# Moving a chunk's down projection between the next chunk's gate and up projections

## The chip, the core and the metric

The kernel runs on one core of a Trainium2 chip. The metric is the device time of one execution in microseconds; lower is better. The engines are named PE (matmul, its weight loads as PEld), DVE (vector), ACT (scalar), POOL (GpSimd) and SP (which issues the loads of weights).

## What is computed

Two blocks follow each other on 512 tokens of 1024 features, in float32. The first has two layers of recurrence, latent attention and memory attention; the second has a feed-forward network, a mixer of neighbourhood attention and pooling, a second feed-forward network and a gated side input. The change touches only the two feed-forward networks:

```python
D_FF = 2816

def swiglu(x, w_gate, w_up, w_down):
    return (jax.nn.silu(x @ w_gate) * (x @ w_up)) @ w_down

def second_block(...):
    f = swiglu(rms_norm(h, ffn1_pre_g[i]), ffn1_w_gate[i], ffn1_w_up[i], ffn1_w_down[i])
    h = h + 0.5 * rms_norm(f, ffn1_post_g[i])
    ...
    f = swiglu(rms_norm(h, ffn2_pre_g[i]), ffn2_w_gate[i], ffn2_w_up[i], ffn2_w_down[i])
    h = h + 0.5 * rms_norm(f, ffn2_post_g[i])
```

## The kernel before

**Precision by splitting.** Every operand is kept as a high and a low part (`xh`, `xl`; `wh`, `wl`), and a product is three matmuls: high by high, high by low, low by high (lines 902 to 904).

**Blocks, pieces, units.** A plan is written out once as a list, and every engine walks through it in order. A `Block` is one projection. Its weights come in units of up to four tiles of 128 rows; its output lies in PSUM banks 0 to 3 (`bank`), and a piece is one unit times one bank, up to 4 x 3 = 12 matmuls. A gate or up block ("tr": the weights are stationary, the activations move) has two units; with 512 columns it has four banks and eight pieces, with 256 columns two banks and four pieces. A down projection is two blocks ("nat": the activations are stationary, the weights move) of one unit and four pieces each, one for each half of the output features. A bank that is filled again waits until the block before has been read out of it (`prior`).

**How weights come.** SP loads a unit into one of two buffers `raw`, ACT casts it to `wh` (line 1255, three buffers) and POOL subtracts the cast from it, which gives `wl` (line 851). ACT casts the unit that is two places ahead of the piece it has come to (`prepare`), and only when the unit before that piece's is over on PE.

**The networks.** The 2816 inner columns are cut into six chunks of 512, 256, 512, 512, 512 and 512 columns. Below, G0 to G5, U0 to U5 and D0 to D5 are their gate, up and down projections. ACT evacuates G with a SiLU to `SG` (line 1276). DVE evacuates U bank by bank in three steps (`times_gate`): the product with `SG` (line 1651), its cast to the high part (line 1652), the low part by subtraction (line 1653). These parts are the stationary operand of D; they are kept in `yh`, `yl` for even chunks and in `zh`, `zl` for odd ones. DVE adds D's banks up in `facc` (line 1647, shown as `side`). A D waits for all evacuations of its U (`need`, by the semaphore `dve_evac`). D0 starts at bank 2 in place of bank 0 (`shift`).

**The order before** is G0 U0 G1 U1 D0 G2 U2 D1 G3 U3 D2 G4 U4 D3 G5 U5 D4, and then D5 within the phase `norm`, in which the root mean square of the sum is taken and the result is transposed (line 1157) for the next block. ACT, DVE and PE enter such a phase by `settle_before`, a wait for all evacuations of the blocks ahead of it.

Of the kernel before, what the change touches and what calls it, by code (L numbers as in the profile page):

```python
# [302 lines left out]
def build(nc, x, x_t, mem_t, positions, w_in, w_uq, w_uk, w_uv, w_mk, w_mv, w_out, ln_g, ln_b, cols_in,  # L303
# [3 lines left out]
    with ctx:  # L307
# [111 lines left out]
        def w_cols(w, row0, ktiles, c0, width):  # L419
            return w[row0:row0 + ktiles * P, c0:c0 + width].rearrange("(k p) n -> p k n", p=P)  # L420

        plan = []
        add = plan.append
# [14 lines left out]
        def norm(first, last_blocks, pre=None, turned=True, scale=1.0, second=True, by_columns=False):  # L438


            _, at = norm_order(first, pre, turned)
            ph = Phase("norm", *(len(o) for o in at), slots=T + 1, writes="x" if turned else None, mode=first,
                       gain=pre, tiles=2 if turned else 0, scale=scale, layer=second)
            ph.by_columns = by_columns
            if len(last_blocks) == 2:
                last_blocks[1].shift = 2
            if first == "layer":

                between, *ends = (b.pieces() for b in last_blocks)
                for b, at in zip(last_blocks, ((0, 1, 0, 1), (2, 2, 0, 2), (3, 3, 1, 3))):  # L450
                    b.shift, b.at = 0, at
                ph.slots[0], ph.slots[2] = between[:2], between[2:]
                for n in range(T):
                    ph.slots[n + 1] += [pieces[n] for pieces in ends]
                add(ph)
                return
            for b in last_blocks:
                pieces = b.pieces()
                ph.slots[0] += pieces[:-T]
                for n in range(T):  # L460
                    ph.slots[n + 1].append(pieces[n - T])
            add(ph)
# [99 lines left out]
        def load_gains(post, pre=None):  # L562
            pairs = [(gain2_b[:, 0, :], post_gains[post:post + 1, :].partition_broadcast(P))]
            if pre is not None:
                pairs.append((gain2_b[:, 1, :], pre_gains[pre:pre + 1, :].partition_broadcast(P)))
            add(Load(*pairs))

        def ffn(wg, wu, wd, gains, by_columns=False):

            widths = [512, D_FF % 512] + [512] * (D_FF // 512 - 1)  # L570
            chunks = [(sum(widths[:i]), width) for i, width in enumerate(widths)]

            def down(i):
                c, width = chunks[i]
                blocks = [Block(w_cols(wd, c, width // P, n * 512, 512), width // P, 512, "nat", f"ff{i % 2}",
                                "accumulate", "dve", (n, i == 0)) for n in range(2)]
                if i == 0:

                    for b in blocks:
                        b.shift = 2  # L580
                return blocks

            for i, (c, width) in enumerate(chunks):
                add(Block(w_cols(wg, 0, KD, c, width), KD, width, "tr", "x", "silu", "act", SG, banks=width // P))
                add(Block(w_cols(wu, 0, KD, c, width), KD, width, "tr", "x", "times_gate", "dve", i % 2,
                          banks=width // P))
                if i == 0:
                    load_gains(*gains)
                else:
                    for b in down(i - 1):  # L590
                        add(b)
            norm("post", down(len(chunks) - 1), pre="work2", scale=0.5, by_columns=by_columns)

        ffn(f1g, f1u, f1d, (0, 1), by_columns=True)


# [48 lines left out]
        add(Phase("turned", writes="x"))  # L645
        norm("post", last[2:], pre="work2")
        ffn(f2g, f2u, f2d, (2, 3))

        load_gains(3)
# [36 lines left out]
        for e in plan:  # L686
# [4 lines left out]
            if isinstance(e, Late):  # L691
                b = e.block
# [12 lines left out]
            for piece in (e.pieces() if isinstance(e, Block) else [pc for slot in e.slots for pc in slot]):  # L705
                b, unit, j = piece
# [1506 lines left out]
```

How the kernel before makes its waits and increments, by code:

```python
        def wait(eng, semaphore, value):  # L757
            if value > 0:
                eng.wait_ge(semaphore, value)
# [1 line left out]
        def units_over(eng, n):  # L761
            if n > 0:
                eng.wait_ge(*unit_end[n - 1])
# [46 lines left out]
        @block.sync  # L811
# [14 lines left out]
                if u == 10:  # L826
                    sp.dma_start(xs[:, :, :], x.rearrange("(t p) n -> p t n", p=P)).then_inc(x_loaded, 16)
                if u >= 2:
                    wait(sp, low_done, low_upto[u - 1][0])
                    wait(sp, low_done_dve, low_upto[u - 1][1])
                sp.dma_start(raw[:, u % 2, 0:nk, 0:b.width], b.w[:, k0:k0 + nk, :]).then_inc(raw_loaded[u % 2], 16)
            for t in range(T):
                for n in range(2):
                    sp.wait_ge(dve_step, finish.dve + 2 + 2 * t + n)
                    cut = slice(n * 512, (n + 1) * 512)
                    sp.dma_start(out[t * P:(t + 1) * P, cut], xs[:, t, cut]).then_inc(stored, 16)
            sp.wait_ge(stored, 16 * 2 * T)
# [2 lines left out]
        @block.gpsimd  # L842
        def _(pool):
            for u, (b, k0, nk) in enumerate(units):
                for k in range(nk):
                    if low_on_dve(u, k):
                        continue
                    pool.wait_ge(high_done, tiles_upto[u] + k + 1)
                    s = (slice(None), u % 3, k, slice(0, b.width))
                    pool.tensor_tensor(wl[s], raw[:, u % 2, k, 0:b.width], wh[s].bitcast(F32),
                                       ALU.subtract).then_inc(low_done, 1)
```

## Time and profile before

| | us |
|---|---|
| median of 3 runs | 2118.03 |
| lowest and highest run | 2116.44, 2118.12 |
| span of the profiled execution | 2113.3 |
| PE busy | 2089.2 |
| DVE busy | 894.8 |
| POOL busy | 868.0 |
| ACT busy | 789.8 |

The page gives the span of the profiled execution, from its first to its last instruction, and not its whole time. Busy times are shares of that span; the four engines run side by side. A matmul's busy time in the trace includes the time in which it drains, so that matmuls in a row overlap: their price is read from the distance between two starts.

### The profile page before, as it was taken

How to read it: one execution, taken by the hardware profiler on the slowest of the kernel's cores; microseconds unless marked ns; L12 is line 12 of the kernel's file. 1: busy time of each engine (PE TensorE's matmuls, PEld its weight loads, DVE VectorE, ACT ScalarE, POOL GpSimd, SP SyncE). 2: the span in 40 equal slices, each digit the busy share in tenths (PEclk: the TensorE clock that was granted, in tenths of full speed). 3: DMA queues.
4: the chain of work that ended last, by engine and by line, in shares of the span. 5: the costliest groups of instructions: out<-in, count | busy, mean ns of one | idle time of the engine just before them, and what ended most of it. 6: DMA issues, size and time to landing. Idle time of an engine off the chain costs nothing.

```text
span 2113.3 us, 33496 instructions
## 1 busy us (share of the span) xinstructions
PE 2089.2 (99%) x13820; PEld 1741.6 (82%) x13820; DVE 894.8 (42%) x1653; ACT 789.8 (37%) x1611; POOL 868.0 (41%) x680
## 2 busy tenths in 40 slices
PE   8999999999999999999999999999999999999998
PEld 7878888778978888778888888888888888888886
DVE  6173565535373465526432211433422612222264
ACT  5424335554423325455422222345433432222244
POOL 4633433232543433233354444343444345454423
PEclk9999999999999999999999999999999999999999
DMA  7522223122222223122242332242233133332222
GB/s 247 178 65 80 78 67 100 41 80 80 80 82 80 77 68 100 41 81 70 76 144 83 118 98 83 89 135 80 66 114 100 61 110 101 109 108 92 100 70 90
DMA packets 98679, 196.65 MB, mean 93 GB/s; under 512 B 3680, under 2 KB 12256, under 8 KB 98144
## 3 DMA queue, kind: packets, MB, share of 16 engines
q1 hardware_dynamic: 95072, 183.25, 26.6%
q10 hardware_dynamic: 3456, 11.27, 1.5%
q8 instruction: 109, 1.79, 0.3%
q14 instruction: 42, 0.34, 0.1%
HBM read 192.41 MB, written 2.10 MB: 92 GB/s over the span
## 4 chain that ended last, share of the span: by engine, by line
PE 59%; ACT 1%; DVE 0%; issue 0%; DVEq 0%
PE ps L902 18%; PE ps L903 18%; PE ps L904 18%; PE ps L1017 1%; PE ps L1157 1%; PE ps L1025 0%; PE ps L1034 0%; PE ps L1180 0%; PE ps L1200 0%; PE ps L1189 0%; PE ps L1070 0%; PE ps L1052 0%; ACT L1581 0%; PE ps L974 0%; PE ps L1210 0%; PE ps L1062 0%
## 5 line engine op out<-in xcount | busy, mean ns | idle before, releaser
L851 POOL TENSOR_TENSOR wl<-raw,wh 128x512 fp32r<-128x512 f32 (+2 forms) x676 | 867.8, 1307 | 1220.6 <-ACT wh L1255 1210.8
L1255 ACT CAST wh<-raw 128x512 fp32r<-128x512 f32 (+2 forms) x692 | 380.7, 604 | 773.3 <-PE ps L904 672.8
L902 PE MATMUL ps<-xh,wh 128*128 128x512 f32 (+1 forms) x1376 | 514.2, 374 | 1.2 <-issue 1.2
L904 PE MATMUL ps<-xh,wl 128*128 128x512 f32 (+1 forms) x1376 | 509.1, 370 | 0.0
L903 PE MATMUL ps<-xl,wh 128*128 128x512 f32 (+1 forms) x1376 | 508.7, 370 | 0.0
L902 PEld LDWEIGHTS ps<-xh,wh 128*128 128x128 f32 x1376 | 259.4, 189 | 46.1 <-issue 3.9
L904 PEld LDWEIGHTS ps<-xh,wl 128*128 128x128 f32 x1376 | 259.1, 188 | 44.6
L903 PEld LDWEIGHTS ps<-xl,wh 128*128 128x128 f32 x1376 | 259.4, 188 | 42.1
L902 PE MATMUL ps<-wh,xh 128*128 128x512 f32 (+1 forms) x608 | 239.1, 393 | 0.2 <-issue 0.2
L904 PE MATMUL ps<-wh,xl 128*128 128x512 f32 (+1 forms) x608 | 234.4, 386 | 0.0
L903 PE MATMUL ps<-wl,xh 128*128 128x512 f32 (+1 forms) x608 | 234.4, 385 | 0.0
L902 PE MATMUL ps<-wh,yh 128*128 128x512 f32 x496 | 198.0, 399 | 0.2
L904 PE MATMUL ps<-wh,yl 128*128 128x512 f32 x496 | 193.6, 390 | 0.0
L903 PE MATMUL ps<-wl,yh 128*128 128x512 f32 x496 | 193.4, 390 | 0.0
L1651 DVE TENSOR_TENSOR work<-ps,work 128x512 f32<-128x512 f32 x44 | 30.3, 688 | 383.3 <-PE ps L904 383.3
L902 PEld LDWEIGHTS ps<-wh,xh 128*128 128x128 f32 x608 | 114.2, 188 | 22.6 <-issue 1.4
L904 PEld LDWEIGHTS ps<-wh,xl 128*128 128x128 f32 x608 | 114.2, 188 | 21.8
L903 PEld LDWEIGHTS ps<-wl,xh 128*128 128x128 f32 x608 | 114.3, 188 | 20.4 <-issue 0.2
L902 PEld LDWEIGHTS ps<-wh,yh 128*128 128x128 f32 x496 | 93.3, 188 | 20.5 <-POOL wl L851 0.8
L904 PEld LDWEIGHTS ps<-wh,yl 128*128 128x128 f32 x496 | 93.1, 188 | 19.9
L903 PEld LDWEIGHTS ps<-wl,yh 128*128 128x128 f32 x496 | 93.3, 188 | 18.5
L1647 DVE TENSOR_TENSOR side<-side,ps 128x512 f32<-128x512 f32 x88 | 59.3, 686 | 106.0 <-PE ps L904 103.4
(273 smaller groups left out, 2436.2 us busy)
## 6 DMA issues: line engine op xcount, KB each, us to landing
raw<-w_in SPq DMA_DIRECT2D x58, 1024.0 KB, 5.2
raw<-w_out SPq DMA_DIRECT2D x20, 1024.0 KB, 5.0
raw<-f1g SPq DMA_DIRECT2D x10, 1024.0 KB, 5.1
raw<-f1u SPq DMA_DIRECT2D x10, 1024.0 KB, 5.1
raw<-f1d SPq DMA_DIRECT2D x10, 1024.0 KB, 5.0
raw<-f2g SPq DMA_DIRECT2D x10, 1024.0 KB, 5.2
raw<-f2u SPq DMA_DIRECT2D x10, 1024.0 KB, 5.1
raw<-f2d SPq DMA_DIRECT2D x10, 1024.0 KB, 5.1
```

Source lines behind the costliest of these rows:

```text
L851: pool.tensor_tensor(wl[s], raw[:, u % 2, k, 0:b.width], wh[s].bitcast(F32), ALU.subtract).then_inc(low_done, 1)
L902: pe.matmul(o, still[0], move[0], start=k0 + k == 0, stop=False)
L903: pe.matmul(o, still[0], move[1], start=False, stop=False)
L904: mm = pe.matmul(o, still[1], move[0], start=False, stop=k0 + k == b.ktiles - 1)
L1017: mm = pe.matmul(ps[:, 4 + h, 0:width], q_heads[:, 2 * p + h, cut], k_heads[:, p, h, 0:width], start=True, stop=True)
L1157: mm = pe.transpose(ps[:, 4 + 2 * (t % 2) + b, f * P:(f + 1) * P], src[:, t, (4 * b + f) * P:(4 * b + f + 1) * P], ident[:, :])
L1255: act.copy(wh[:, v % 3, k, 0:width], raw[:, v % 2, k, 0:width]).then_inc(high_done, 1)
L1647: ins = dve.tensor_copy(dst, src) if first else dve.tensor_tensor(dst, dst, src, ALU.add)
L1651: link(dve.tensor_tensor(tmp, src, SG[:, j, :], ALU.mult))
```

## The change

In the loop over chunks, D of the chunk before is added behind the gate projection in place of behind the up projection. The order becomes G0 U0 G1 D0 U1 G2 D1 U2 G3 D2 U3 G4 D3 U4 G5 D4 U5, and then D5 within the norm. Blocks, pieces, banks, units and buffers stay as they are; only their order changes, on every engine that walks through the plan.

```diff
             for i, (c, width) in enumerate(chunks):
                 add(Block(w_cols(wg, 0, KD, c, width), KD, width, "tr", "x", "silu", "act", SG, banks=width // P))
+                for b in down(i - 1) if i else ():
+                    add(b)
                 add(Block(w_cols(wu, 0, KD, c, width), KD, width, "tr", "x", "times_gate", "dve", i % 2,
                           banks=width // P))
                 if i == 0:
                     load_gains(*gains)
-                else:
-                    for b in down(i - 1):
-                        add(b)
             norm("post", down(len(chunks) - 1), pre="work2", scale=0.5, by_columns=by_columns)
```

In the following rows a name pair is output, moving operand, stationary operand. The new file is one line shorter ahead of the matmuls, so lines 902 to 904 become 901 to 903. PE at the end of the first network, where D5 (`zh`, `zl` stationary) begins, before:

```order
L902 MATMUL ps<-wh,yh 128x512
L903 MATMUL ps<-wl,yh 128x512
L904 MATMUL ps<-wh,yl 128x512
L902 MATMUL ps<-wh,zh 128x512 [waits low_done,dve_evac]
L903 MATMUL ps<-wl,zh 128x512
```

and with the change:

```order
L901 MATMUL ps<-xh,wh 128x512
L902 MATMUL ps<-xl,wh 128x512
L903 MATMUL ps<-xh,wl 128x512
L901 MATMUL ps<-wh,zh 128x512 [waits low_done,dve_evac]
L902 MATMUL ps<-wl,zh 128x512
```

Before, the last matmuls of D4 stand ahead of D5's first; now the last ones of U5 do, whose evacuations write `zh` and `zl`.

PE behind U1, the up projection with two banks, before (the last three matmuls of U1, the first two of D0, which begins on bank 2):

```order
L902 MATMUL ps<-xh,wh 128x512
L903 MATMUL ps<-xl,wh 128x512
L904 MATMUL ps<-xh,wl 128x512
L902 MATMUL ps<-wh,yh 128x512 [waits low_done,dve_evac]
L903 MATMUL ps<-wl,yh 128x512
```

and with the change (the last three of U1, the first two of G2, which begins on bank 0):

```order
L901 MATMUL ps<-xh,wh 128x512
L902 MATMUL ps<-xl,wh 128x512
L903 MATMUL ps<-xh,wl 128x512
L901 MATMUL ps<-xh,wh 128x512 [waits dve_evac,low_done,dve_step,act_step]
L902 MATMUL ps<-xl,wh 128x512
```

D0 has moved ahead of U1, and G2 follows U1 directly, on the two banks that U1 has just filled.

## Rows read from the trace of the kernel before

**Rows 1.** The page's first part: busy us, share of the span, instructions.

```profile
PE 2089.2 (99%) x13820; PEld 1741.6 (82%) x13820; DVE 894.8 (42%) x1653; ACT 789.8 (37%) x1611; POOL 868.0 (41%) x680
```

**Rows 2.** Both networks: stretch, length, busy PE, PEld, DVE, ACT, POOL, clock, DMA.

```profile
1015.00:1357.00 342.00, 342.00 (x1604) 286.59 (x1604) 89.14 (x124) 87.96 (x168) 163.00 (x133) 1.00 0.32 102
1683.00:2025.00 342.00, 342.00 (x1603) 286.64 (x1604) 89.34 (x123) 88.12 (x168) 163.18 (x133) 1.00 0.31 102
```

**Rows 3.** PE's timeline: start, us, instruction. First matmuls of U1 and of D0.

```profile
1072.31 0.39 PE L902 MATMUL ps<-xh,wh 128*128 128x512 f32 x1
...
1083.19 0.39 PE L902 MATMUL ps<-wh,yh 128*128 128x512 f32 x1
```

**Rows 4.** DVE's timeline: U1's two banks, U5's last bank, D4's last; brackets: idle before.

```profile
1080.77 0.69 DVE L1651 TENSOR_TENSOR work<-ps,work 128x512 f32<-128x512 f32 x1 [17.26 <-PE ps L904]
1081.50 1.29 DVE L1652 CAST zh<-work 128x512 fp32r<-128x512 f32 x1
1082.82 1.66 DVE L1653 TENSOR_TENSOR zl<-work,zh 128x512 fp32r<-128x512 f32 x1
...
1086.22 1.66 DVE L1653 TENSOR_TENSOR zl<-work,zh 128x512 fp32r<-128x512 f32 x1
...
1334.68 0.69 DVE L1651 TENSOR_TENSOR work<-ps,work 128x512 f32<-128x512 f32 x1 [0.79 <-PE ps L904]
1335.41 0.43 DVE L1652 CAST zh<-work 128x512 fp32r<-128x512 f32 x1
1335.87 1.67 DVE L1653 TENSOR_TENSOR zl<-work,zh 128x512 fp32r<-128x512 f32 x1
...
1356.45 0.69 DVE L1647 TENSOR_TENSOR side<-side,ps 128x512 f32<-128x512 f32 x1 [2.04 <-PE ps L904]
```

**Rows 5.** PE's timeline: the first matmul of D4, one within the norm phase.

```profile
1334.48 0.39 PE L902 MATMUL ps<-wh,yh 128*128 128x512 f32 x1
...
1381.03 0.36 PE L902 MATMUL ps<-xh,wh 128*128 128x256 f32 x1 [0.44 <-issue]
```

**Rows 6.** DVE's timeline: cast and subtraction of a bank of U0.

```profile
1054.30 0.43 DVE L1652 CAST yh<-work 128x512 fp32r<-128x512 f32 x1
1054.76 0.69 DVE L1653 TENSOR_TENSOR yl<-work,yh 128x512 fp32r<-128x512 f32 x1
```

**Rows 7.** POOL's timeline: subtractions in a row, around U1 and at D4's start.

```profile
1073.69 10.24 POOL L851 TENSOR_TENSOR wl<-raw,wh 128x512 fp32r<-128x512 f32 x8 [1.42 <-ACT wh L1255]
...
1335.44 5.75 POOL L851 TENSOR_TENSOR wl<-raw,wh 128x512 fp32r<-128x512 f32 x4 [5.67 <-ACT wh L1255]
```

**Rows 8.** ACT's timeline: casts at D4's start, and those in the norm phase.

```profile
1334.74 2.19 ACT L1255 CAST wh<-raw 128x512 fp32r<-128x512 f32 x4 [8.70 <-PE ps L904]
...
1357.45 2.18 ACT L1255 CAST wh<-raw 128x512 fp32r<-128x512 f32 x4 [9.64 <-issue]
```

**Rows 9.** Timeline of DVE and PE: a matmul elsewhere that waited for DVE.

```profile
973.68 0.69 DVE L1878 TENSOR_TENSOR work<-ps,work 128x512 f32<-128x512 f32 x1 [0.62 <-PE ps L1070]
...
974.51 0.45 PE L1070 MATMUL ps<-work,side 128*128 128x256 f32 x1 [0.34 <-DVE work L1878]
```

**Rows 10.** PE's timeline at the kernel's start.

```profile
7.95 0.58 PE L902 MATMUL ps<-yh,wh 128*128 128x256 f32 x1 [7.95 <-POOL wl L851]
8.32 0.42 PE L903 MATMUL ps<-yl,wh 128*128 128x256 f32 x1
...
16.16 0.38 PE L902 MATMUL ps<-yh,wh 128*128 128x256 f32 x1
16.37 0.28 PE L903 MATMUL ps<-yl,wh 128*128 128x256 f32 x1
16.49 0.28 PE L904 MATMUL ps<-yh,wl 128*128 128x256 f32 x1
```

**Rows 11.** Windows at the kernel's end, columns as in rows 2.

```profile
2105.00:2106.00 1.00, 0.97 (x5) 0.47 (x3) 0.29 (x1) 0.95 (x4) 0.00 (x0) 1.00 0.23 86
2108.00:2109.00 1.00, 0.00 (x0) 0.00 (x0) 1.00 (x2) 0.46 (x3) 0.00 (x0) 0.86 0.00 0
```

## The prediction

> **What bounds the kernel now.** I read the page's first part for the busiest engine, then the windows over the two feed-forward networks, then the timelines of PE, DVE and POOL at the two places where the new order puts blocks side by side that were apart.
>
> PE is busy for 2089.2 of 2113.3 us [rows 1]. In the two windows that hold the networks, from the first matmuls of the gate projection to the first ones of the last down projection, it is busy for 342.00 of 342.00 us, both times, at a granted clock of 1.00 [rows 2]. That is the main fact: where the change acts, PE does not wait at all. Weight loads, casts on ACT, subtractions on POOL and evacuations on DVE are all hidden behind matmuls. A reordering there cannot shorten anything that PE waits for; it can only keep PE full or open gaps. The number and the shapes of the matmuls stay what they are: U1 runs from 1072.31 to 1083.19 [rows 3], 48 matmuls at 0.2267 us, so a piece of 12 takes 2.72 us, and I take the same price for it in its new place.
>
> So the question is which new neighbours make PE wait. I call G, U and D the gate, up and down projection of chunk i, and T the moment at which an up projection's last piece is over and the next block's first matmul starts in the trace of before.
>
> **Edits that cost nothing, and their cover.** D(i-1) behind G(i) needs all four (or two) evacuations of U(i-1); in the new order a whole G lies between them, 21.8 us for a chunk of 512 and 10.9 us for the one of 256 (that of U1). DVE ends the last of them about 2 us after U's end, so this is covered several times over. U(i) behind D(i-1) starts on a bank that was filled three pieces before; behind the shifted D0 its first bank was filled one piece, 2.72 us, earlier, and a down evacuation takes 0.69 us [rows 4]. G(i+1) behind a four-bank U(i) starts on a bank that was filled three pieces, 8.2 us, before. The units keep their sizes, and each is still cast while the unit two places ahead of it runs; the two short units of G1 and the two of U1 now stand apart, which gives SP's loads, ACT's casts and POOL's subtractions more room, not less. No instruction is added on any queue, and the load of gains stays behind U0. Sum: 0.
>
> **Term 1: D5 directly behind U5 (both networks).** D5's first matmul waits for all four evacuations of U5, since its stationary operand is what they write. Before, D4 with 21.8 us lay between. Now the last bank's evacuation is exposed. In the trace U5 ends at T = 1334.48 [rows 5]; DVE takes up bank 3 at 1334.68, its product lasts 0.69, its cast starts at 1335.41 and its subtraction at 1335.87 [rows 4]. The start was set by PE (DVE had been idle for 0.79 us before it), so this start stays. The subtraction took 1.67 us there. Where POOL is idle it takes 0.69 [rows 6], and POOL had begun four subtractions at 1335.44 [rows 7]. That burst belongs to the unit that ACT began to cast at 1334.74, as soon as D4 began [rows 8]. In the new place the next unit belongs to the block behind the norm, and ACT reaches it only when the norm phase's settling wait is over, that is after the last evacuation of the block ahead: in before this is seen as the cast at 1357.45 [rows 8], 0.31 us behind the end of D4's last evacuation (1356.45 + 0.69) [rows 4]. So POOL will not be running and I take 0.69: bank 3 is ready at 1335.87 + 0.69 = 1336.56, T + 2.08. From DVE's end to PE's start I take 0.14 us (973.68 + 0.69 = 974.37 to 974.51) [rows 9], and 0.15 us because the first matmul after a wait has its weight load exposed (7.95 to 8.32 is 0.37 where the spacing is 0.21) [rows 10]. Term 1 is 2.08 + 0.14 + 0.15 = 2.37 us per network. Its bounds: 2.2 without the last surcharge, 3.4 if POOL runs after all (1.67 in place of 0.69).
>
> **Term 2: G2 directly behind U1 (both networks).** U1 has only two banks. Behind it, D0 used its two other banks first; G2 uses bank 0 first, which was filled one piece, 2.72 us, before U1's end. In the trace U1 ends at T = 1083.19 [rows 3]. DVE starts bank 0 at 1080.77, but the cast takes 1.29 and the subtraction 1.66, so that it ends at 1084.48, T + 1.29 [rows 4]; the second network shows the same pattern. The reason is POOL: it ran eight subtractions from 1073.69 for 10.24 us, to 1083.93 [rows 7], 1.28 each, while the same cast and subtraction take 0.43 and 0.69 where it is idle [rows 6]. Is POOL there in the new order too? The casts for the two units of G2 start when the two units of U1 start, as those for D0's did: a burst of four from about U1's start + 1, another from its second unit's start + 1 (1072.31 + 5.44 + 0.96 = 1078.7) to about 1083.8. The second burst lies on bank 0's evacuation as before, so I take the measured end. G2 then starts at T + 1.29 + 0.14 + 0.15 = T + 1.58 in place of T. Its second piece needs bank 1 at T + 1.58 + 2.72 = T + 4.30. In before bank 1 was ready at 1086.22 + 1.66 = 1087.88, T + 4.69 [rows 4], with the handing over T + 4.98: 0.68 more. POOL's third burst is shorter in the new order (D1's unit has two tiles, not four), so bank 1 may come up to 0.5 us earlier; I take half of the 0.68. Term 2 is 1.58 + 0.34 = 1.92 us. Its bounds: 0, if DVE has POOL out of its way (1.88 us of work from 1080.77 end at 1082.65, ahead of T), and 2.3.
>
> The Trainium skill (SBUF — State Buffer, "Who interferes with whom") says that DVE and GpSimd share a port pair, which whoever starts first keeps for the whole instruction while the other waits. By that rule a cast and a subtraction could each have to sit out one whole POOL subtraction of 1.28 us, in place of the 0.86 and 0.97 us seen here; bank 0 would end 0.73 us later, and the sum, as an estimate by that page, would be 2 x 0.73 = 1.5 us more. What the trace has is in between, as it should be where the second engine comes while the first is under way.
>
> **Sum.** 2.37 + 1.92 = 4.29 us per network, 8.6 us for two. The page gives the span of the profiled execution, 2113.3 us, and not its own time; the median of the three runs is 2118.03, 4.7 us above, which I take for what lies around the span. I add to the median: 2126.6 us, 0.4% slower. The bounds of the terms give 2 x 2.2 = 4.4 and 2 x 5.7 = 11.4: 2122.4 to 2129.4.
>
> **Rivals.** *Only the last wait is left, not slower.* If POOL's second burst in U1 ends ahead of bank 0's cast (the point is 1081.50 on the clock of before, T - 1.69), or starts behind it, term 2 is 0. Term 1 leaves 4.7 us, and if the norm behind D5 swallows its own short wait (0.44 us on PE [rows 5]) it gives back 0.9: 2118.0 + 4.7 - 0.9 = 2121.8, within 0.2%, which is about what a measurement of this kernel can tell from no change (4.2 us, the line at 2122.3). Without the gift it is 2122.7. For it: the neighbouring units change, and POOL's bursts follow them. Against it: the burst hangs on the start of U1's second unit, which keeps its distance to the bank.
>
> *The clock falls.* At the start of the kernel, after 7.95 us of idle PE, matmuls of 256 columns are spaced 0.21 us until 16.37 and 0.12 after it [rows 10], the two levels of 1.2 and 2.4 GHz. At the end, PE stops at 2106 and the granted clock is 0.86 in the slice from 2108 to 2109 [rows 11]. PE would be idle for about 2.1 us in front of D5. If that were enough, up to 8.4 us would run at half speed, up to 4 us lost per network; with half of it 2126.6 + 4 = 2130.6. Against it: the clock still held more than 2 us behind PE's last matmul.
>
> The Trainium skill (TensorE: Matmul & The Clock Gate, "A second HAM failure mode: psum-queue depth-cycling") tells of a kernel whose short PE pauses between groups of matmuls made the clock swing between its two levels. By it the new waits, which are such pauses, would cost the price of this rival. The trace speaks against it: the windows that hold the networks are at 1.00, but they hold no pause either.
>
> *A gain.* It would need PE time to win back, and there are 0.00 us of it in 684 [rows 2]. I keep a small chance for what I don't see. That the change does nothing is excluded by PE's order.
>
> **How the numbers follow.** Forecast, both waits: 0.72, 2124 to 2129.4. Only the last wait: 0.15, 2121.8 to 2122.8. The clock: 0.09, 2129 to 2134. A gain: 0.04. Predicted 2126.6. For 8 in 10 the range reaches from 2121.8 to 2130.2; it leaves out the gain and most of the clock's case. Slower by over 0.2%: 0.72 + 0.09 + a little over a quarter of the second case, 0.85; within 0.2%: 0.11; faster: 0.04.
>
> **What would show it.** PE's waits of the new profile should hold two waits on DVE of about 2 us at the first matmul of D5, behind the up projection's subtraction, and two of about 1.3 us at G2's first matmul, perhaps two short ones at its second piece; PE's busy time in the networks unchanged; clock 1.00. Wrong would be: no wait at G2 (second case), a wait at D5 well over 2.5 us (POOL was there), matmuls behind it spaced wider than 0.23 us (the clock), or a PE wait on POOL or on a load anywhere in the networks, which would mean that the order of units matters after all.

## The result and the profile after

The changed kernel takes 2124.89 us (median of 4 runs, 2124.29 to 2127.45) against 2117.24 us for the kernel before on the same chip (4 runs, 2116.24 to 2118.12): ratio 1.0042, 95% interval 1.0029 to 1.0056. It is slower by 0.4%, as forecast (2126.6, range 2121.8 to 2130.2). A second, larger comparison gave 1.0043 (below).

PE's waits of the changed kernel, longest in total first (what it waited for: us in total, times, longest):

```profile
PE ps L901 <- POOL wl L850: 9.0, 3, 7.6
PE ps L901 <- DVE zl L1652: 6.7, 4, 2.0
PE ps L1093 <- DVE work L1942: 2.5, 2, 1.3
```

The second line is new: four waits for the up projection's subtraction, which the kernel before has not at all. They are the two forecast ones, once in each network. PE's idle time in the networks, 0.00 us before [rows 2], is 3.3 us in each now (346.00 less 342.67 and 342.68; the windows are 4 us longer because the networks are, and the idle time is the waits' 1.36 + 1.97):

```profile
1015.00:1361.00 346.00, 342.67 (x1603) 286.16 (x1602) 89.46 (x122) 88.98 (x169) 161.88 (x134) 1.00 0.31 101
1687.00:2033.00 346.00, 342.68 (x1601) 286.21 (x1600) 89.78 (x123) 88.74 (x169) 161.86 (x134) 1.00 0.31 101
```

**G2 behind U1.** DVE's timeline (start, us, instruction, idle before) around the end of U1 in the first network:

```profile
1102.13 0.69 DVE L1650 TENSOR_TENSOR work<-ps,work 128x512 f32<-128x512 f32 x1 [7.57 <-PE ps L903]
1102.86 1.27 DVE L1651 CAST zh<-work 128x512 fp32r<-128x512 f32 x1
1104.17 1.65 DVE L1652 TENSOR_TENSOR zl<-work,zh 128x512 fp32r<-128x512 f32 x1
...
1107.28 1.66 DVE L1652 TENSOR_TENSOR zl<-work,zh 128x512 fp32r<-128x512 f32 x1
```

POOL's at the same time:

```profile
1100.07 5.20 POOL L850 TENSOR_TENSOR wl<-raw,wh 128x512 fp32r<-128x512 f32 x4 [0.41 <-ACT wh L1254]
1105.51 2.88 POOL L850 TENSOR_TENSOR wl<-raw,wh 128x512 fp32r<-128x512 f32 x2 [0.24 <-ACT wh L1254]
```

PE's, with U1's last matmul, G2's first, and the step to G2's second piece (1109.00):

```profile
1104.33 0.39 PE L903 MATMUL ps<-xh,wl 128*128 128x512 f32 x1
1106.08 0.47 PE L901 MATMUL ps<-xh,wh 128*128 128x512 f32 x1 [1.36 <-DVE zl L1652]
1106.38 0.40 PE L902 MATMUL ps<-xl,wh 128*128 128x512 f32 x1
...
1108.69 0.39 PE L903 MATMUL ps<-xh,wl 128*128 128x512 f32 x1
1109.00 0.50 PE L901 MATMUL ps<-xh,wh 128*128 128x512 f32 x1
1109.33 0.40 PE L902 MATMUL ps<-xl,wh 128*128 128x512 f32 x1
```

Cast and subtraction of U1's bank 0 are as slow as before [rows 4], POOL's second burst lies over them as before [rows 7], and bank 0 is ready at 1104.17 + 1.65 = 1105.82. G2 starts 0.26 us later. Without a wait it would have started at 1104.33 + 0.227 = 1104.56, so the start is 1.52 us late; the first matmul takes 0.07 more than usual. The second piece starts 0.08 late (0.31 us behind the matmul before it, in place of 0.23), since bank 1 was ready only at 1107.28 + 1.66 = 1108.94, and its first matmul takes 0.10 more than usual; the third burst was short, as the order of units said. The rest is spread thinly: behind its first matmul, the matmuls of G2's first piece are 0.231 us apart in place of 0.227. Over the 144 matmuls of U1 and G2 the trace holds 1.86 us more than 144 x 0.2267 us, and 1.87 in the second network.

**D5 behind U5.** The last bank of U5 on DVE:

```profile
1357.90 0.69 DVE L1650 TENSOR_TENSOR work<-ps,work 128x512 f32<-128x512 f32 x1 [0.79 <-PE ps L903]
1358.62 0.43 DVE L1651 CAST zh<-work 128x512 fp32r<-128x512 f32 x1
1359.08 0.69 DVE L1652 TENSOR_TENSOR zl<-work,zh 128x512 fp32r<-128x512 f32 x1
```

and PE, with U5's last matmul and D5's first two:

```profile
1357.47 0.39 PE L903 MATMUL ps<-xh,wl 128*128 128x512 f32 x1
1359.83 0.50 PE L901 MATMUL ps<-wh,zh 128*128 128x512 f32 x1 [1.97 <-DVE zl L1652]
1360.17 0.39 PE L902 MATMUL ps<-wl,zh 128*128 128x512 f32 x1
```

POOL is out of the way here: ACT begins the next unit's cast at 1360.08 and POOL its subtractions at 1360.78, both behind the evacuation, which therefore takes 0.69 at its last step in place of 1.67 [rows 4]:

```profile
1360.78 5.05 POOL L850 TENSOR_TENSOR wl<-raw,wh 128x512 fp32r<-128x512 f32 x4 [7.80 <-ACT wh L1254]
```

The evacuation ends at 1359.77; PE starts at 1359.83, 2.13 us behind the free slot at 1357.70, and spends 0.11 more than usual on the first matmul: 2.24 us.

**The clock, in the second network only.** Windows of 1 us around D5's start there (stretch, length, busy of PE, PEld, DVE, ACT and POOL, granted clock, DMA):

```profile
2030.00:2031.00 1.00, 0.08 (x1) 0.00 (x0) 0.85 (x2) 0.00 (x0) 0.00 (x0) 1.00 0.00 0
2031.00:2032.00 1.00, 0.00 (x0) 0.00 (x0) 0.96 (x2) 0.00 (x0) 0.00 (x0) 1.00 0.00 0
2032.00:2033.00 1.00, 0.95 (x2) 0.83 (x3) 0.00 (x0) 0.70 (x2) 0.00 (x1) 0.52 0.00 0
2033.00:2034.00 1.00, 1.00 (x4) 0.73 (x3) 0.00 (x0) 1.00 (x3) 1.00 (x1) 0.50 0.00 0
2034.00:2035.00 1.00, 1.00 (x4) 0.81 (x3) 0.00 (x0) 0.48 (x1) 1.00 (x2) 0.50 0.00 0
2035.00:2036.00 1.00, 1.00 (x4) 0.80 (x4) 0.00 (x0) 0.00 (x0) 1.00 (x2) 0.77 0.00 0
2036.00:2037.00 1.00, 1.00 (x6) 0.79 (x5) 0.21 (x1) 0.00 (x0) 1.00 (x2) 1.00 0.00 0
```

and PE's timeline within it:

```profile
2032.05 0.79 PE L901 MATMUL ps<-wh,zh 128*128 128x512 f32 x1 [1.97 <-DVE zl L1652]
...
2033.07 0.63 PE L903 MATMUL ps<-wh,zl 128*128 128x512 f32 x1
2033.50 0.63 PE L901 MATMUL ps<-wh,zh 128*128 128x512 f32 x1
```

The granted clock falls to 0.5, the lower of its two levels (1.2 GHz), as the matmuls come back after a wait of 1.97 us, and stays there for 3.4 us; matmuls are 0.43 us apart in place of 0.23. The first 60 matmuls of D5 take 1.64 us more than 60 x 0.2333, of which 0.11 is the first one: the fall costs 1.53 us. In the first network the same wait, to the hundredth, left the clock at 1.00 (D5 starts at 1359.83):

```profile
1360.00:1361.00 1.00, 1.00 (x5) 0.82 (x6) 0.00 (x0) 0.92 (x2) 0.22 (x1) 1.00 0.00 0
```

Together: 1.86 + 1.87 + 2 x 2.24 + 1.53 = 9.7 us in the networks. The span grew by 9.2 (2113.3 to 2122.5); the kernel reached the first network 0.4 us earlier in this execution than in the one before.

### The profile page after: what moved, and what is told of

It is laid out like the page before. It is cut to its first block, busy times and chain, and to the rows that moved or that the text cites. A ratio compares the mean times of both kernels' runs of the same rounds, so it can differ in the third digit from the quotient of the medians.

```text
span 2122.5 us, 33496 instructions
## 1 busy us (share of the span) xinstructions
PE 2091.6 (99%) x13820; PEld 1741.3 (82%) x13820; DVE 895.0 (42%) x1653; ACT 790.0 (37%) x1611; POOL 866.0 (41%) x680
## 4 chain that ended last, share of the span: by engine, by line
PE 58%; DVE 1%; ACT 1%; issue 0%; DVEq 0%
PE ps L901 18%; PE ps L902 18%; PE ps L903 18%; PE ps L1016 1%; PE ps L1156 1%; PE ps L1024 0%; PE ps L1033 0%; PE ps L1179 0%; PE ps L1199 0%; PE ps L1188 0%; PE ps L1069 0%; PE ps L1051 0%; DVE zl L1652 0%; ACT L1580 0%; PE ps L973 0%
```

## The experiments

The theory was: the new order costs nothing by itself; it exposes two evacuations in each network, U1's (bank 0, slowed by POOL) in front of G2 and U5's in front of D5, and behind D5's wait the clock may fall. The rivals were that every moved D costs a little, that POOL has nothing to do with U1's evacuation, that something other than these evacuations holds PE, and that the new order has a gain that the waits hide. The cover of an evacuation, below, is the time that other matmuls fill between it and the block that needs it. All ratios are to runs of the kernel before on the same chip, with a 95% interval behind them; a difference in us is worked out from the ratio. Line numbers shift a little from kernel to kernel.

**The changed kernel again** (label e1_again).

> The changed kernel once more, as the yardstick for the others. Theory (each network loses 1.9 us at G2, which waits for U1's evacuation, and 2.2 us at D5, which waits for U5's; on top of it the clock falls behind one of the D5 waits for 1.5 us): 7 to 9.5 us slower than the kernel before, and four waits of PE on the up projection's subtraction, two of 1.3 to 1.4 and two of about 2.0 us. If the fall of the clock is a matter of chance, it may be behind the first network's D5 this time, behind both, or behind none.

2124.51 us (5 runs) against 2116.00 (24 runs), ratio 1.0043, interval 1.0030 to 1.0055: 9.1 us. The four waits were there with the same lengths, and the clock fell behind neither D5. It did fall elsewhere: at 48 us, in the first block's start, where PE had waited 2.39 us for weights (see the last section).

**D4 alone back** (e2_last_back).

```diff
-                for b in down(i - 1) if i else ():
+                for b in down(i - 1) if i and i not in (5,) else ():
                     add(b)
                 add(Block(w_cols(wu, 0, KD, c, width), KD, width, "tr", "x", "times_gate", "dve", i % 2,
                           banks=width // P))
+                for b in down(i - 1) if i in (5,) else ():
+                    add(b)
```

> D4 alone goes back behind U5; D0 to D3 stay in their new places. Theory: the two waits in front of D5 are gone, and with them the fall of the clock; what stays is the wait at G2, 2 x 1.9 = 3.7 us slower than the kernel before (3 to 5). Rival, that the new order costs by itself (every D between G and U a little): 6 or more.

1.0018 (1.0009 to 1.0027), 3.8 us. The waits in front of D5 are gone, the two at G2 stay (1.36 us each, 1.89 and 1.86 us with what hangs on them). PE's waits on the up projection's subtraction in this kernel (us in total, times, longest):

```profile
PE ps L903 <- DVE zl L1654: 2.7, 2, 1.4
```

**D0 alone back** (e3_first_back): the same edit with `(1,)` in place of `(5,)`.

> D0 alone goes back behind U1; D1 to D4 stay in their new places. Theory: the two waits at G2 are gone; what stays is 2 x 2.2 = 4.5 us in front of D5 and the clock's 1.5 us or so, 4.5 to 6 us slower than the kernel before, or more if the clock falls twice. Rival, that the clock's fall needs both kinds of waits: 4.5 and granted clock 1.00 behind D5.

1.0025 (1.0015 to 1.0035), 5.3 us. The waits at G2 are gone; those in front of D5 stay, and in the profile the clock fell behind the second one. So the fall does not need the waits at G2.

```profile
PE ps L903 <- DVE zl L1654: 3.9, 2, 2.0
```

The two kernels' losses add up: 3.8 + 5.3 = 9.1 us, the loss of the whole change. Each of the two has an interval of about 2 us to either side, so that the sum fits to the tenth is luck.

**Both back** (e4_both_back): with `(1, 5)`; D1, D2 and D3 stay between gate and up.

> D0 and D4 go back, D1 to D3 stay between gate and up. Theory: no wait in either network, time of the kernel before within 1 us. Rival, that the moves in the middle cost or bring something too: off by more than 2 us on either side.

1.0003 (0.9994 to 1.0012): no difference. PE's waits from 1014 to 1390 us of this kernel are two of 0.4 us in the norm phases, as in the kernel before [rows 5]:

```profile
PE ps L903 <- issue: 0.8, 2, 0.4
```

The three moves in the middle are free, in both directions.

**G2's banks in another order** (e5_g2_shift).

```diff
                 add(Block(w_cols(wg, 0, KD, c, width), KD, width, "tr", "x", "silu", "act", SG, banks=width // P))
+                plan[-1].shift = 2 if i == 2 else 0
```

> The changed kernel with G2's banks taken in the order 2, 3, 0, 1, as D0's are; nothing else. Theory: G2's first two pieces find free banks, U1's evacuation has two more pieces (5.4 us) of cover, and the wait at G2 is gone: about 3.7 us faster than the changed kernel, 4.5 to 6 slower than the kernel before. Rival, that G2 waits for something else that comes in at the same time (its weights' subtraction): a wait of 1.4 us stays at its first matmul, by another name.

1.0028 (1.0016 to 1.0041), 5.9 us. The waits in front of D5 make 4.5 of it, and in the profile the clock fell behind both. The waits at G2 are gone although D0 stays ahead of U1:

```profile
PE ps L902 <- DVE zl L1653: 3.9, 2, 2.0
```

It was the bank, and nothing else that came in at the time. The windows at D5's start in the second network (columns as above) show one thing more:

```profile
2030.00:2031.00 1.00, 0.70 (x3) 0.61 (x4) 0.25 (x1) 0.44 (x1) 0.00 (x0) 1.00 0.00 0
2031.00:2032.00 1.00, 1.00 (x6) 0.79 (x5) 0.00 (x0) 1.00 (x3) 0.75 (x1) 0.88 0.00 0
2032.00:2033.00 1.00, 1.00 (x4) 0.81 (x3) 0.00 (x0) 0.73 (x2) 1.00 (x2) 0.50 0.00 0
```

D5 starts at 2030.30, and the clock still holds 1.00; it falls 1.5 us later, with PE at work again. In four of the six falls behind these waits (both of this kernel, one each of e3 and e7) it fell 0.8 to 1.5 us behind D5's first matmul, and in the other two just as that matmul began.

**Half of D4 as cover** (e6_half_down).

```diff
-                for b in down(i - 1) if i else ():
+                before_up = down(i - 1) if i else []
+                for b in before_up[:1] if i == 5 else before_up:
                     add(b)
                 add(Block(w_cols(wu, 0, KD, c, width), KD, width, "tr", "x", "times_gate", "dve", i % 2,
                           banks=width // P))
+                if i == 5:
+                    add(before_up[1])
```

> The changed kernel with one half of D4 (its second block, 10.9 us) behind U5 and the other half still ahead of it. Theory: half a down projection is cover enough for an exposed evacuation of 2.1 us; no wait in front of D5, no fall of the clock, 3 to 5 us slower than the kernel before (the wait at G2 stays). Rival, that the whole of D4 is needed: some of the 2 us stays.

1.0017 (1.0007 to 1.0026), 3.6 us, which is what the two waits at G2 cost (1.88 + 1.86); in front of D5 there is none. Ten microseconds of other matmuls between U5 and D5 do as well as twenty.

**POOL out of the way at U1** (e7_thin_lows). Left out are the low parts of 504 of 512 columns in two units of each network.

```diff
-                    s = (slice(None), u % 3, k, slice(0, b.width))
-                    pool.tensor_tensor(wl[s], raw[:, u % 2, k, 0:b.width], wh[s].bitcast(F32),
+                    n = 8 if b.thin and (k0 or b.evac == "accumulate") else b.width
+                    s = (slice(None), u % 3, k, slice(0, n))
+                    pool.tensor_tensor(wl[s], raw[:, u % 2, k, 0:n], wh[s].bitcast(F32),
...
+                blocks[0].thin = i == 1
...
                 add(Block(w_cols(wg, 0, KD, c, width), KD, width, "tr", "x", "silu", "act", SG, banks=width // P))
+                plan[-1].thin = i == 2
```

> The changed kernel in which POOL subtracts only 8 of 512 columns for two units per network, the second one of G2 and the first one of D1, whose subtractions run while U1's banks are evacuated; the low parts of these units are left wrong. Theory: with POOL out of the way the cast takes 0.43 and the subtraction 0.69 us, bank 0 is ready about 0.5 us ahead of U1's end, and G2 does not wait: the two waits of 1.4 us are gone. Rival, that DVE is slow there for another reason (its own chain, ACT's casts, the matmuls): casts of 0.8 to 1.3 and subtractions of 1.66 us, and the waits stay.

One run, 2120.96 us. The waits at G2 are gone; those in front of D5 stay, and the clock fell behind the second one. U1's bank 0 on DVE in this kernel:

```profile
1102.06 0.69 DVE L1654 TENSOR_TENSOR work<-ps,work 128x512 f32<-128x512 f32 x1 [7.57 <-PE ps L907]
1102.78 0.43 DVE L1655 CAST zh<-work 128x512 fp32r<-128x512 f32 x1
1103.24 0.69 DVE L1656 TENSOR_TENSOR zl<-work,zh 128x512 fp32r<-128x512 f32 x1
```

Cast and subtraction take 0.43 and 0.69 us where they took 1.27 and 1.65. POOL's subtractions were the cause, and without them a cover of one piece (2.72 us) is enough for an evacuation of 1.87 us.

**A longer wait in front of D5** (e8_long_pause). DVE does the last subtraction four times over, writing the same values.

```diff
+                    for _ in range(3 if b.last and j == 3 else 0):
+                        link(dve.tensor_tensor(ol[:, j, :], tmp, oh[:, j, :].bitcast(F32), ALU.subtract))
                     ins = dve.tensor_tensor(ol[:, j, :], tmp, oh[:, j, :].bitcast(F32), ALU.subtract)
...
                 add(Block(w_cols(wu, 0, KD, c, width), KD, width, "tr", "x", "times_gate", "dve", i % 2,
                           banks=width // P))
+                plan[-1].last = i == 5
```

> The changed kernel in which DVE repeats the last subtraction of U5's last bank three times more, which adds about 3 x 0.73 = 2.2 us to the wait in front of D5. Theory: PE's idle time there goes from 2.0 to about 4.2 us in each network, and the granted clock falls to half behind both: 4.4 us of wait and 1.5 to 4 us more for each fall that was not there. Rival, that the fall in the second network has nothing to do with the wait's length: it stays there and the first network stays at 1.00.

One run, 2131.64 us. The waits are 4.15 us and the clock fell in both networks. In the first one (windows, columns as above) it fell while PE still waited:

```profile
1360.00:1361.00 1.00, 0.00 (x0) 0.00 (x0) 0.93 (x3) 0.00 (x0) 0.00 (x0) 0.91 0.00 0
1361.00:1362.00 1.00, 0.00 (x0) 0.00 (x0) 0.97 (x2) 0.00 (x0) 0.00 (x0) 0.50 0.00 0
...
1367.00:1368.00 1.00, 1.00 (x4) 0.77 (x4) 0.10 (x1) 0.00 (x0) 1.00 (x1) 0.68 0.00 0
```

That one lasted 6.8 us, the first 1.5 of them within the wait, and cost 2.4 us behind it; the one in the second network cost 1.6. Two falls behind two waits are also what an even chance gives one time in four, so that the longer wait makes the fall more likely fits this run and is not shown by it. The rival's sign, a first network that stays at 1.00, did not come.

**Waiting tile by tile** (e9_by_tile). D5's first tile of 128 rows is U5's bank 0, its second one bank 1, and so on; only the first piece's last three matmuls need bank 3.

```diff
-                        wait(pe, dve_evac, b.need[1])
+                        wait(pe, dve_evac, b.need[1] - (3 if b.ktiles == 4 and j == 0 else 0))
...
                 for k in range(nk):
+                    if b.need[0] == "evac" and b.ktiles == 4 and j == 0 and k:
+                        wait(pe, dve_evac, b.need[1] - 3 + k)
```

> The changed kernel with its order as it is, but a down projection's first piece waits for the up projection's evacuations tile by tile (its first three matmuls for bank 0, the next three for bank 1, and so on), not for all four at once. Theory: bank 3 is ready 2.1 us behind U5's end and is wanted by the tenth matmul, 9 x 0.233 = 2.1 us behind it, so the wait in front of D5 shrinks from 2.0 us to 0.2 or less, the clock does not fall there, and only the waits at G2 are left: 3 to 5 us slower than the kernel before. Rival, that something other than the evacuation holds D5 back: a wait of about 2 us stays, by whatever name.

1.0018 (1.0009 to 1.0028), as with D4 back in its old place. PE at D5's tenth matmul, the first to need bank 3:

```profile
1362.37 0.39 PE L905 MATMUL ps<-wh,zl 128*128 128x512 f32 x1
1362.63 0.49 PE L903 MATMUL ps<-wh,zh 128*128 128x512 f32 x1
1362.96 0.40 PE L904 MATMUL ps<-wl,zh 128*128 128x512 f32 x1
```

and the subtraction of bank 3 on DVE:

```profile
1361.88 0.69 DVE L1654 TENSOR_TENSOR zl<-work,zh 128x512 fp32r<-128x512 f32 x1
```

Bank 3 was ready at 1361.88 + 0.69 = 1362.57. The tenth matmul starts 0.26 us behind the ninth and takes 0.33: 0.13 us lost in place of 2.24, and the clock stays at 1.00 behind it.

**Both covered, the new order kept** (e10_by_tile_shift): e9 and e5 together.

> The same, and G2 takes its banks in the order 2, 3, 0, 1. All five down projections stay between gate and up. Theory: both waits are covered, and the new order costs nothing: within 1 us of the kernel before. If the new order held a gain that the waits hid, this kernel would be faster than the one before by more than 1 us.

0.9996 (0.9986 to 1.0005): the kernel before, within the measurement. PE is busy for 342.00 of 342.00 us in both networks, as in [rows 2]:

```profile
1015.00:1357.00 342.00, 342.00 (x1604) 286.48 (x1603) 88.55 (x123) 88.08 (x167) 161.91 (x133) 1.00 0.32 102
1683.00:2025.00 342.00, 342.00 (x1604) 286.52 (x1604) 88.76 (x121) 88.05 (x168) 162.09 (x133) 1.00 0.31 102
```

So the new order by itself neither costs nor gains, as far as the interval (3 us faster to 1 us slower) can tell; none of the versions here is faster than the kernel before.

**The clock once more** (e11_third_look), the changed kernel unaltered.

> The changed kernel a third time, for the clock behind D5 alone. Of ten waits of about 2.0 us in front of D5 in five profiles, five let the clock fall. Theory, chance: the four waits are there with the same lengths as before, and the clock falls behind none, one or both of the D5 waits; behind the two waits of 1.4 us at G2 it stays at 1.00.

One run, 2124.44 us. The four waits had the same lengths; this time the clock fell behind D5 in the first network (1.52 us) and not in the second.

## Why the prediction was right

**The bound.** PE had nothing to win back in the networks. e4 and e10 bear this out from two sides: with the waits gone, three or five moved down projections make no difference.

**The edits that cost nothing** cost nothing (e4, e10). There was no wait of PE on POOL or on a load in the networks, in any of these profiles.

**Term 1, D5.** Forecast 2.37 us, measured 2.24. Each link came as read: DVE's start is set by PE, POOL is away, bank 3 is ready at T + 2.07. Of the surcharges, 0.14 for the way from DVE to PE was 0.06, and 0.15 for the first matmul was 0.11.

**Term 2, G2.** Forecast 1.92, measured 1.86 and 1.87. The measured end of bank 0's evacuation carried over (T + 1.26 against T + 1.29), because the burst on POOL hangs on the start of U1's second unit, as argued; the longer case, in which cast and subtraction each sit out a whole subtraction on POOL, did not come (they took 0.84 and 0.96 us more than where POOL is idle). The other parts are less exact than their sum. The way from DVE to PE took 0.26 against 0.14, the first matmul 0.07 against 0.15, and the second piece waited 0.08 for its bank where 0.34 was added; against that stand 0.19 us that the forecast did not have, in the second piece's first matmul and in matmuls a little wider apart. That the term is right to 0.06 us is luck in part. The rival without term 2 names the right mechanism: e7 takes POOL away and the term goes.

**The clock** is where the forecast was too mild. Its chance was put at 0.09, against it stood that the clock had held for more than 2 us behind the kernel's last matmul [rows 11], and the text expected 1.00 behind D5. In six profiles with waits of 1.97 us in front of D5 the clock fell behind 6 of 12, and nothing that these profiles show told beforehand which. The price was put at up to 4 us for each, from the 8.4 us at the kernel's start; a fall lasts 3.4 us here and costs 1.5. So the rival came true in half of the cases, at about a third of its highest price: 0.8 us for each network on average, which the sum did not have. The end of the kernel was one instance, and I read it as a bound.

The Trainium skill (TensorE: Matmul & The Clock Gate, "A second HAM failure mode: psum-queue depth-cycling") tells of a kernel whose frequent short pauses between groups of matmuls made the clock swing between its two levels. The traces agree in so far as single pauses of 2 us let it fall (6 of 12); those of 1.36 us at G2 did not (none of 14, each of which cost 1.86 to 1.89 us in all).

**The sum.** Forecast 8.6 us of waits; the profile holds 8.2 of waits and 1.5 of clock, and the ratio of the larger comparison is 9.1 us (interval 6.3 to 11.6). That 8.6 lies so near to it is luck in part: the waits were put 0.4 us too high, and the clock adds 1.5 us on average. The forecast took 4.7 us for what lies around the span; it is 1.8 (2124.29 less 2122.5). This did no harm, since the sum was added to the median, but the 4.7 should have told that the profiled execution of before was a quicker one than the median.

## What to carry to other kernels

Where PE is never idle, read a reordering as a question of cover alone: for each consumer that gets a new neighbour, set the producer's last evacuation, with the contention it meets in that place, against the work now in between. A consumer that waits for all of its operand at once can be made to wait for it tile by tile, and a block that follows a short one can start on the banks that the short one does not use; each of these took a whole term away here. And a wait of about 2 us on PE can cost more than its length, because the clock may fall behind it: here 1.5 us more in six of twelve cases.

## What was not expected of the hardware

**Equal pauses of 2 us let PE's clock fall in half of the cases.** Behind six of twelve pauses of 1.97 us the granted clock was at 0.5 for 3.4 us, at 1.5 us each; it fell at both pauses of 4.15 us, at 2.4 and 1.6 us; at none of fourteen pauses of 1.36 us, nor at the two of 1.26 to 1.31 us that each of the thirteen profiles holds at some 130 and 610 us. What decides among equal pauses isn't settled by these runs.

**The start of the kernel can hold such a pause too, with or without the change.** In e1_again PE waits at 46 us for weights that come late:

```profile
48.07 0.47 PE L901 MATMUL ps<-wh,yh 128*128 128x512 f32 x1 [2.39 <-POOL wl L850]
```

and the clock falls behind it; in the profile of before there is no such wait, and in that of the changed kernel it is 0.71 us. The profiles of e2, e6 and e9 hold it too (1.99, 2.15 and 1.77 us), and the clock fell at each. In these four profiles PE reaches its matmuls at some 901 us 2.3 to 3.3 us later than in the other nine. The times of a kernel lie in two groups: eight of e6's ten are 2118.87 to 2119.27 us, and its profiled execution, with the wait, is one of the other two (2121.26). The times of the kernel before (2114.5 to 2118.5 in all comparisons) are grouped in the same way, some 2.5 us apart. So the wait and its fall fit the spread; that they are its cause was not tried.
